# A tile's gates added into the table by indirect DMAs, and a longer lead

## The chip, the cores and the metric

The kernel runs on one core of a Trainium2 chip. The metric is the device time in microseconds; the other cores of the chip are not used.

## The reference

One transformer block over 512 tokens of width 1024, in float32. First a mixer: modulation by a conditioning vector, sliding-window attention of 8 heads beside an mLSTM of 4 heads, an output projection and a residual. Then the part that takes most of the time, the PEER layer: every token picks 128 of 16384 experts (16 in each of 8 heads).

```python
q = (ht @ w_q).reshape(T, 8, 2, 128)
s1, s2 = einsum(q[:, :, 0], keys1), einsum(q[:, :, 1], keys2)   # (T, 8, 128) each
v1, i1 = top_k(s1, 16); v2, i2 = top_k(s2, 16)
cand = v1[..., :, None] + v2[..., None, :]                      # 256 a head
top, pos = top_k(cand, 16)
eidx = (i1 * 128 + i2) at pos                                   # experts, distinct within a head
gate = softmax(top)
act = gelu(einsum('thkd,td->thk', u[eidx], ht)) * gate
y = einsum('thk,thkd->td', act, v[eidx])
```

`u` and `v` are tables of 16384 rows of 1024 floats, 64 MB each. Two heads of a token may choose the same expert; their gates then add up. A second residual with a modulated norm ends the block.

## The kernel before

The first part (up to line 1350) is the mixer and the query scores. `peer_block`, line 1353, is the rest. It splits the tokens. For 192 of them (tile 0 and half of tile 1) the rows of `u` and `v` that they chose are gathered from HBM by indirect DMAs, a row for each of 128 partitions at a time: 384 gathers of 512 KB (`NROWS`), each followed by one VectorE instruction, a dot product for `u` (L1798), a multiply-add for `v` (L1807). The gathers are issued by GpSimd at L1527 into a ring of six buffers, each when VectorE has finished the row six before.

For the other 320 tokens (`TD`, the hot tokens) TensorE computes with all experts. The tables are cut into 128 blocks of 128 experts. A u block is transposed (L1641, L1703) and multiplied with the tokens in three products of split floats: high half with high and low half of the tokens (L1656), low half with the high one (L1660). ScalarE takes the gelu of the scores (L1551). That is multiplied with the gates of the block, a dense table of 128 experts by 320 tokens that is zero where an expert was not chosen, and goes against the v block (L1716 to L1731).

The work is laid out in turns. In the **lead**, turns 0 to 55 (`LEAD` = 56), there are only u blocks; their gelu goes to a table in HBM (`gelu_table`). In the **middle**, turns 56 to 127, each turn does a u block and a v block. In the **tail**, turns 128 to 185, the v blocks that belong to the lead are done, with gelu rows read back (`s_in`). So every block taken into the lead adds one turn to the lead and one to the tail and takes one from the middle.

The lead is long since the gates must be ready before the first v block. VectorE searches the four tiles of 128 tokens one after the other (`for t in range(NT)`), each with the order of its instructions written out, and between them puts the work of the turns by a planner's clock (`beside`, `lead_block`). `SEL_AT` says at which turn a tile's gates are settled. The gates of the hot tokens are then made by TensorE: `turn_choice` transposes keys and gates of a tile, `hot_rows` (VectorE, L1834 and L1838) builds one-hot rows for four tokens, `gates` (TensorE, L1668) multiplies them into a 128 by 128 table for each of the four tokens, `stage_gates` (ScalarE, L1558) copies it, and SP stores it to `gate_table` in HBM (L1468). There are 80 such steps (`GSTEPS`), spread over turns 27 to 50. From there SP loads the gates of eight blocks at a time (L1457) into two buffers.

The low half of a u block in the lead is made in one of two ways: TensorE subtracts the high half in PSUM (L1649) and ScalarE copies, or VectorE subtracts (L1845), for the turns in `LOW_BY_DVE`. `ROWS_LEAD` and `ROWS_TAIL` say how many of the gathered rows are taken in lead and tail: 34 and 68; the middle has the other 282. On SP's queue (L1460 to L1507) stand, in order, u loads, table stores, v loads, gate and gelu loads, each behind its wait, in rings of four.

Of the kernel before, what the change touches and what calls it, by code (L numbers as in the profile page):

```python
# [59 lines left out]
GSTEPS = TD // GT  # L60
TB = 20
NTB = TD // TB
BG = 8
NBG = NBLK // BG
# [24 lines left out]


def tile_of(m):
    return 1 if m < STEPS_OF[1] else 2 if m < STEPS_OF[1] + STEPS_OF[2] else 3

# [7 lines left out]
def gate_steps():  # L101

    steps, m = [[] for _ in range(LEAD)], 0
    ends = {1: SEL_AT[2], 2: SEL_AT[3], 3: G_END}
    for t in (1, 2, 3):
        for it, n in spread(STEPS_OF[t], range(SEL_AT[t] + 1, ends[t] + 1)).items():
            steps[it] = list(range(m, m + n))
            m += n
    return steps


def rows_by_turn():

    n = dict.fromkeys(range(END), 0)
    n |= spread(ROWS_LEAD[0], range(SEL_AT[0] + 2, SEL_AT[3] + 1))
    n |= spread(ROWS_LEAD[1], range(SEL_AT[3] + 1, G_END + 2))
# [5 lines left out]
STEPS, ROWS_AT = gate_steps(), rows_by_turn()  # L122
TURN_OF = [turn for turn in range(END) for _ in range(ROWS_AT[turn])]
# [69 lines left out]
def mix_block(nc, A, keep, R_dram):  # L193

    x_sb, hT, ident, cols, gg2 = keep["x"], keep["hT"], keep["ident"], keep["cols"], keep["gg2"]
    with ExitStack() as ctx:
# [48 lines left out]
        mod_sum = sb("mod_sum", [P, 4, 512])  # L245
        bias_if = sb("bias_if", [MH, 2])
# [60 lines left out]
        block = ctx.enter_context(nc.Block())  # L307

# [93 lines left out]
        def _(pool):  # L402
# [9 lines left out]
            nc.gpsimd.memset(zeros, 0.0).then_inc(S["consts"], 1)  # L412
            nc.gpsimd.memset(v_ext[:, :, :, MV:MV + 1], 1.0).then_inc(S["consts"], 1)
# [18 lines left out]
        CONSTS = 5  # L432
# [920 lines left out]
def peer_block(nc, A, keep, s_all, S_dram, G_dram, out):  # L1353
# [4 lines left out]
    with ExitStack() as ctx:  # L1358
# [6 lines left out]
        def sems(name, n):  # L1365
# [16 lines left out]
        gbuf = stage.rearrange("p g i t -> p g (i t)").rearrange("p g (q b t) -> p g q b t", q=NTB, b=BG)  # L1382
# [15 lines left out]
        chosen_u = sb("chosen_u", [P, 2, K], U32)  # L1398
        tsum = sb("tsum", [P, 2, NT, PH])
        sel = sb("sel", [P, NT - 1, 2, K])  # L1400
        selT = keep["lot"][:, 2 * NBLK * TB:2 * NBLK * TB + 3 * TD].rearrange("p (i t) -> p i t", i=3)
# [47 lines left out]
        def _(sp):  # L1449
# [11 lines left out]
            for it in range(LEAD):  # L1461
# [48 lines left out]
        def _(pool):  # L1510
            nc.gpsimd.iota(iota_i[:], pattern=[[1, P]], base=0, channel_multiplier=0).then_inc(iota_ready, 1)
            pool.wait_ge(eidx_ready, 1)
            for j in range(NROWS):
                if j == EIDX_B_AT:

                    pool.wait_ge(eidx_ready, 2)
                    pool.dma_start(eidx[NB:P, K:K + KB], chosen_u[0:NB, 0, KB:K]).then_inc(eidx_b_in, 16)
                if j == K:
                    pool.wait_ge(eidx_b_in, 16)
                if j == K + 1:  # L1520

                    pool.wait_ge(sel_ready, 2)
# [8 lines left out]
        def _(act):  # L1531
# [33 lines left out]
            func(minus_one[:], ident[:], ACT.Copy, scale=-1.0).then_inc(consts, 1)  # L1565
            lead_high(0)
            lead_low(0)
            for it in range(LEAD):
# [5 lines left out]
                for t in range(NT):  # L1574
                    if it == SEL_AT[t] - 1:
                        act.wait_ge(top_ready, t + 1)
# [5 lines left out]
            for n in range(LEAD, END):  # L1582
# [3 lines left out]
                if n < NBLK:  # L1586
                    act.wait_ge(half_turned, n - LEAD + 1)
                    act.wait_ge(u_done, n)
                    func(H[:, 0, 0:512], ps[:, 6 + n % 2, :], ACT.Copy).then_inc(ua_high, 1)
# [35 lines left out]
        def _(pe):  # L1625
# [19 lines left out]
            def lead_less(n):  # L1645

                pe.wait_ge(u_high, n + 1)
# [24 lines left out]
            def turn_choice(t):  # L1672

                pe.wait_ge(sel_ready, t + 1)
# [6 lines left out]
            pe.wait_ge(consts, 1)  # L1681
            lead_turn(0)
            lead_less(0)
            for it in range(LEAD):
                if it + 1 < LEAD:
                    lead_turn(it + 1)
                pe.wait_ge(u_high, it + 1)
# [9 lines left out]
                for t in range(1, NT):  # L1697
# [37 lines left out]
            for n in range(LEAD, END):  # L1735
# [14 lines left out]
                if n < NBLK:  # L1750
                    pe.wait_ge(ua_high, n - LEAD + 1)
                    pe.wait_ge(ub_high, n - LEAD + 1)
                    pe.wait_ge(ua_low, n - LEAD + 1)
                    scores_high(6 + n % 2, 0)
                    pe.wait_ge(ub_low, n - LEAD + 1)
# [8 lines left out]
        def _(dve):  # L1764
            v = nc.vector
            step = Chain(dve, chain)
            dve.wait_ge(iota_ready, 1)
            step(v.tensor_copy(iota[:], iota_i[:]))
# [41 lines left out]
            def settle(t):  # L1810

                tops, s = top[:, t, :, :], lambda i: tsum[:, i, t, :]
                dve.wait_ge(gate_exp, t + 1)
# [27 lines left out]
            def lead_low(n):  # L1841

                b = n % 2
                dve.wait_ge(u_high, n + 1)
# [215 lines left out]
```

## Time and profile before

| | us |
|---|---|
| median of three runs | 1567.31 (1566.09 to 1570.01) |
| span of the profiled execution | 1563.7 |
| TensorE busy | 1512.8 (97%) |
| VectorE busy | 1401.7 (90%) |
| ScalarE busy | 596.5 (38%) |
| GpSimd busy | 493.3 (32%) |
| moved by DMA | 455.71 MB, mean 291 GB/s |

The span runs from the first to the last instruction of one execution; the profile gives that execution no time of its own beside it. The shares are means over stages with different limits, so they are read again stage by stage. The kernel's three stages of blocks begin at about 392, 742 and 1330 us.

### The profile page before, as it was taken

The numbers are of one execution on the slowest core, as the hardware profiler recorded it, in microseconds if no ns is written. First come the engines' busy times: TensorE is split into PE (matmuls) and PEld (weight loads), VectorE is DVE, ScalarE is ACT, GpSimd is POOL, SyncE is SP. The second block draws the span as 40 slices with busy tenths as digits, with TensorE's granted clock in tenths as the row PEclk, the third lists the DMA queues.
The fourth block names the chain that finished last, engine by engine and source line by source line (L and its number), as shares of the span: only waits on it lengthen the run. The fifth ranks groups of instructions, "written<-read, shape, count | busy, mean of one in ns | idle before, by whom it ended". The sixth has DMA issues, their size and how long they took to land.

```text
span 1563.7 us, 23267 instructions
## 1 busy us (share of the span) xinstructions
PE 1512.8 (97%) x8404; PEld 1281.7 (82%) x8404; DVE 1401.7 (90%) x2988; ACT 596.5 (38%) x968; POOL 493.3 (32%) x422
## 2 busy tenths in 40 slices
PE   7999999899999999999999999999999999999996
PEld 5455654788899999999898999999999899787885
DVE  5887987799999999995999999999999999989997
ACT  3104431521555445543333333333333333334343
POOL 1000000232010411010555565555555555343330
PEclk9999999999999999999999999999999999999998
DMA  9864232230465788789999999999999999999993
GB/s 325 287 217 148 101 138 59 81 98 38 136 212 154 261 262 256 251 278 313 408 396 396 402 401 410 407 397 398 399 407 404 385 402 375 362 406 377 398 391 121
DMA packets 180570, 455.71 MB, mean 291 GB/s; under 512 B 15020, under 2 KB 81700, under 8 KB 178280
## 3 DMA queue, kind: packets, MB, share of 16 engines
q1 hardware_dynamic: 113600, 231.84, 41.2%
q0 software_dynamic: 57632, 209.78, 34.9%
q10 hardware_dynamic: 9224, 12.62, 2.4%
q8 instruction: 67, 1.10, 0.3%
q14 instruction: 47, 0.39, 0.1%
HBM read 421.63 MB, written 32.25 MB: 290 GB/s over the span
## 4 chain that ended last, share of the span: by engine, by line
PE 55%; DVE 13%; DMA 4%; issue 2%; ACT 1%; DVEq 0%; SPq 0%; POOL 0%; ACTq 0%; POOLq 0%
PE peer_psum L1656 13%; PE peer_psum L1660 7%; PE peer_psum L1716 6%; PE peer_psum L1723 6%; PE peer_psum L1731 6%; PE peer_psum L1668 4%; PE peer_psum L1703 3%; PE peer_psum L1720 3%; PE peer_psum L1726 3%; DVE s_all L1807 2%; DMA s_all<-in_peer_v 2%; PE peer_psum L1641 1%; DVE s_all L1902 1%; DVE s_in L1906 1%; DVE s_all L1904 1%
## 5 line engine op out<-in xcount | busy, mean ns | idle before, releaser
L1656 PE MATMUL peer_psum<-hH,hi_slots 128*128 128x320 f32 x1024 | 307.3, 314 | 5.1 <-ACT hi_slots L1599 2.1
L1656 PE MATMUL peer_psum<-hL,hi_slots 128*128 128x320 f32 x1024 | 302.0, 309 | 0.0
L1527 POOL DMA_INDIRECT hT<-in_peer_u,eidx x128 | 146.6, 1145 | 292.0 <-DVE dots L1798 251.5
L1563 ACT ACTIVATE hi_slots<-s_all 128x1024 fp32r<-128x1024 f32 x128 | 135.9, 1062 | 189.2 <-PE peer_psum L1731 172.0
L1527 POOL DMA_INDIRECT hT<-in_peer_v,eidx x128 | 149.6, 1169 | 177.6 <-DVE s_all L1807 164.7
L1656 PEld LDWEIGHTS peer_psum<-hH,hi_slots 128*128 128x128 f32 x1024 | 192.6, 188 | 9.7 <-issue 5.2
L1656 PEld LDWEIGHTS peer_psum<-hL,hi_slots 128*128 128x128 f32 x1024 | 192.6, 188 | 3.1 <-issue 0.2
L1660 PE MATMUL peer_psum<-hH,lo_slots 128*128 128x320 f32 x1024 | 171.2, 309 | 2.1 <-DVE lo_slots L1845 2.1
L1935 DVE TENSOR_TENSOR lo_slots<-s_all,hi_slots 128x1024 fp32r<-128x1024 f32 x128 | 156.3, 1221 | 17.5 <-ACT hi_slots L1563 15.9
L1807 DVE SCALAR_TENSOR_TENSOR s_all<-hT,coef,s_all 128x1024 f32<-128x1024 f32 x126 | 161.3, 1280 | 3.3 <-DMA hT<-in_peer_v,eidx 2.9
L1660 PEld LDWEIGHTS peer_psum<-hH,lo_slots 128*128 128x128 f32 x1024 | 156.6, 188 | 5.1 <-DVE lo_slots L1845 2.6
L1798 DVE CUSTOM_DVE_ANT_0 hT<-hT,lot 128x1024 f32<-128x1024 f32 x128 | 155.8, 1219 | 2.2 <-DMA hT<-in_peer_u,eidx 2.1
L1716 PE MATMUL peer_psum<-hi_slots,a_hi_lo 128*128 128x512 f32 x512 | 147.0, 408 | 4.7 <-ACT a_hi_lo L1596 4.7
L1551 ACT ACTIVATE s_all<-peer_psum 128x320 f32<-128x320 f32 x128 | 56.1, 438 | 244.5 <-PE peer_psum L1660 237.6
L1731 PE MATMUL peer_psum<-lo_slots,a_hi_lo 128*128 128x512 f32 x512 | 140.1, 394 | 0.0
L1723 PE MATMUL peer_psum<-hi_slots,a_hi_lo 128*128 128x512 f32 x512 | 140.1, 394 | 0.0
L1723 PEld LDWEIGHTS peer_psum<-hi_slots,a_hi_lo 128*128 128x128 f32 x512 | 99.0, 193 | 20.9
L1731 PEld LDWEIGHTS peer_psum<-lo_slots,a_hi_lo 128*128 128x128 f32 x512 | 99.0, 193 | 20.4
L1527 POOL DMA_INDIRECT more_rows<-in_peer_u,eidx x64 | 73.7, 1151 | 132.0 <-DVE dots L1798 128.9
L1596 ACT ACTIVATE a_hi_lo<-s_all 128x320 fp32r<-128x320 f32 x128 | 63.7, 497 | 128.9 <-DVE s_all L1961 98.5
L1716 PEld LDWEIGHTS peer_psum<-hi_slots,a_hi_lo 128*128 128x128 f32 x512 | 93.5, 194 | 21.4 <-issue 4.5
L1527 POOL DMA_INDIRECT more_rows<-in_peer_v,eidx x64 | 76.7, 1199 | 67.3 <-DVE s_all L1807 61.2
(318 smaller groups left out, 2856.6 us busy)
## 6 DMA issues: line engine op xcount, KB each, us to landing
ring<-in_peer_u SPq DMA_DIRECT2D x128, 512.0 KB
s_all<-in_peer_v SPq DMA_DIRECT2D x128, 512.0 KB
gate_table<-lot SPq DMA_DIRECT2D x16, 1280.0 KB, 7.1
lot<-gate_table SPq DMA_DIRECT2D x16, 1280.0 KB
gelu_table<-s_all ACTq DMA_DIRECT2D x56, 160.0 KB
s_in<-gelu_table SPq DMA_DIRECT2D x56, 160.0 KB
x_sb<-in_w_mod POOLq DMA_DIRECT2D x8, 1024.0 KB, 8.2
lot<-in_peer_wq SPq DMA_DIRECT2D x8, 1024.0 KB, 5.6
```

Of the source, the lines that this page charges most:

```text
L1527: pool.indirect_dma_start(rows_of(j), None, A[table][0], bass.IndirectOffsetOnAxis(eidx[:, k:k + 1], 0)).then_inc(rows_in[j % RG], 16)
L1563: func(H[:, slot_of(w), :], vb[:, w % RING, :], ACT.Copy).then_inc(v_hi, 1)
L1596: func(aHL[:, w % 2, :, 0], a[:, w % 2, :], ACT.Copy).then_inc(a_hi, 1)
L1656: mm(ps[:, bank, 0:TD], H[:, b, c * P:(c + 1) * P], h[:, c, T0:T], start=(c == 0 and h is hH), stop=False)
L1660: last = mm(ps[:, bank, 0:TD], L[:, b, c * P:(c + 1) * P], hH[:, c, T0:T], start=False, stop=(c == DC - 1))
L1668: last = mm(ps[:, 6 + m % 2, :].rearrange("p (i t) -> p t i", t=GT)[:, k, :], onehot[:, m % NHOT, k, 0, :], onehot[:, m % NHOT, k, 1, :], ...
L1716: mm(y_bank(g, h), aH[:, NB + g * P:NB + (g + 1) * P], H[:, s, h * 512:(h + 1) * 512], start=first, stop=False)
L1723: mm(y_bank(g, h), aL[:, NB + g * P:NB + (g + 1) * P], H[:, s, h * 512:(h + 1) * 512], start=False, stop=False)
L1731: last = mm(y_bank(g, h), aH[:, NB + g * P:NB + (g + 1) * P], L[:, s, h * 512:(h + 1) * 512], start=False, stop=final)
L1798: v.tensor_tensor_reduce(out=rows_of(j), in0=rows_of(j), in1=(h_rows if j < K else keep["h_rows_b"]), scale=1.0, scalar=0.0, op0=ALU.mult, ...
L1807: v.scalar_tensor_tensor(out=y0[:, i, :], in0=rows_of(j), scalar=c, in1=y0[:, i, :], op0=ALU.mult, op1=ALU.add).then_inc(row_done, 1)
L1935: v.tensor_tensor(L[:, s, :], vb[:, w % RING, :], H[:, s, :].bitcast(F32), ALU.subtract).then_inc(v_lo, 1)
```

## The change

Tile 3 is searched first (order 3, 0, 1, 2), and its gates no longer go through the one-hot products. Its part of `gate_table` is filled with zeros during the mixer, VectorE computes for each of its 128 x 128 choices the place in the table, and GpSimd adds the gates there with 128 indirect DMAs of 128 single floats, between its gathers. Within a head the places are distinct; between heads GpSimd waits until all earlier adds have landed. The steps fall from 80 to 48, the lead grows from 56 to 72 blocks, 62 rows are taken in the lead, 97 in the tail and 225 in the middle. The table is stored in pieces of 16 tokens instead of 20.

```diff
-TB = 20
+TB = 16
+SCATTERED = (3,)
+HOT_TOKENS = NB + (SCATTERED[0] - 2) * P
+GSTEPS = HOT_TOKENS // GT
+NTB_HOT = HOT_TOKENS // TB
-LEAD = 56
-SEL_AT = {0: 12, 1: 26, 2: 32, 3: 39}
+LEAD = 72
+SEL_ORDER = (3, 0, 1, 2)
+SEL_AT = {3: 11, 0: 19, 1: 27, 2: 40}
-LOW_BY_DVE = [n for n in range(LEAD) if 25 <= n < 35 or n >= 40]
+LOW_BY_DVE = [n for n in range(LEAD) if 28 <= n < 32 or n >= 41]
-ROWS_LEAD, ROWS_TAIL = (24, 10), 68
+ROWS_LEAD, ROWS_TAIL = (28, 34), 97
-FIN = NBLK + 4
+FIN = NBLK + 27
-STEPS_OF = {1: NB // GT, 2: P // GT, 3: P // GT}
-EIDX_B_AT = RG
+STEPS_OF = {t: (NB if t == 1 else P) // GT for t in range(1, SCATTERED[0])}
+EIDX_B_AT = 16
+ADDS_FIRST = 20
+ADDS_AT = {j: ADDS_FIRST if j == 0 else (K - ADDS_FIRST) * j // (ROWS_IN_LEAD - 1) - (K - ADDS_FIRST) * (j - 1) // (ROWS_IN_LEAD - 1)
+           for j in range(ROWS_IN_LEAD)}
...
+            nc.gpsimd.memset(nothing[:], 0.0).then_inc(S["consts"], 1)
...
+            pool.wait_ge(S["consts"], CONSTS)
+            for g in range(NBG):
+                span = (NTB - NTB_HOT) * BG * TB
+                pool.dma_start(G_table[g, :, NTB_HOT:NTB, :].rearrange("p q n -> p (q n)").rearrange("p (k n) -> p k n", n=512),
+                               nothing[:].unsqueeze(1).broadcast_to([P, span // 512, 512])).then_inc(keep["g_zeroed"], 16)
...
-                if it == G_END + 2:
-                    for i in range(2):
-                        sp.wait_ge(g_stored[i], 16 * (NTB // 2))
-                    load_g(0)
                 if it >= LEAD - 2:
                     sp.wait_ge(g_full, GSTEPS)
                     load_v(it - LEAD + 2)
 
             for w in range(2, RING):
                 load_v(w)
+            for i in range(2):
+                sp.wait_ge(g_stored[i], 16 * (NTB_HOT // 2))
+            for t in SCATTERED:
+                sp.wait_ge(g_added[t], 16 * K)
+            load_g(0)
             load_g(1)
...
+            def add_gates(n):
+
+                nonlocal added
+                for _ in range(n):
+                    h, k = added // PTOP, added % PTOP
+                    if k == 0 and h:
+                        pool.wait_ge(g_added[t], 16 * PTOP * h)
+                    pool.indirect_dma_start(G_flat, bass.IndirectOffsetOnAxis(g_index[:, 0, added:added + 1], 0),
+                                            top[:, t, h, k:k + 1], None, compute_op=ALU.add).then_inc(g_added[t], 16)
+                    added += 1
+
+            pool.wait_ge(keep["g_zeroed"], 16 * NBG)
+            pool.wait_ge(sel_ready, SEL_ORDER.index(t) + 1)
+            add_gates(ADDS_AT[0])
             pool.wait_ge(eidx_ready, 1)
             for j in range(NROWS):
+                if j:
+                    add_gates(ADDS_AT.get(j, 0))
...
+                    if t in SCATTERED:
+                        span = GROUP_SPAN - BG * TB
+                        part = lambda op, by: step(v.tensor_scalar(chosen_u[:, 1, :], ids, by, None, op))
+                        part(ALU.bitwise_and, PK - 1)
+                        step(v.tensor_scalar(g_place[:], chosen_u[:, 1, :], float(NTB * BG * TB), lane_at[:, 0:1], ALU.mult, ALU.add))
...
+                        part(ALU.logical_shift_right, 7)
+                        step(v.scalar_tensor_tensor(out=g_place[:], in0=chosen_u[:, 1, :], scalar=float(TB), in1=g_place[:],
+                                                    op0=ALU.mult, op1=ALU.add))
+                        part(ALU.logical_shift_right, 10)
+                        step(v.scalar_tensor_tensor(out=g_place[:], in0=chosen_u[:, 1, :], scalar=float(span), in1=g_place[:],
+                                                    op0=ALU.mult, op1=ALU.add))
+                        step(v.tensor_copy(g_index[:, SCATTERED.index(t), :], g_place[:]))
```

Left out here: the same search order on the other engines, semaphores that were merged (`ua_high` and `ub_high` into `half_high`, the low ones likewise, with the same waits), a separate tile for the experts of tile 1, and five small instructions at VectorE's start that compute each partition's place.

## Rows read from the trace of the kernel before

**Rows 1.** The page, part 2: busy tenths of TensorE and GB/s, 40 slices.

```profile
PE   7999999899999999999999999999999999999996
...
GB/s 325 287 217 148 101 138 59 81 98 38 136 212 154 261 262 256 251 278 313 408 396 396 402 401 410 407 397 398 399 407 404 385 402 375 362 406 377 398 391 121
```

**Rows 2.** Windows by stage: us; busy us of each engine (instructions); granted clock, DMA share, GB/s.

```profile
392.00:742.00 350.00, 340.73 (x2508) 333.83 (x2509) 317.88 (x951) 172.94 (x236) 46.51 (x42) 1.00 0.73 236
742.00:1330.00 588.00, 582.86 (x3438) 530.17 (x3437) 561.87 (x802) 221.14 (x364) 323.93 (x283) 1.00 1.01 399
1330.00:1560.00 230.00, 216.88 (x920) 175.05 (x918) 207.28 (x274) 90.05 (x130) 77.52 (x62) 0.99 0.90 345
```

**Rows 3.** Timeline of TensorE in the lead, lines of L1660: start us, us.

```profile
400.80 1.34 PE L1660 MATMUL peer_psum<-hH,lo_slots 128*128 128x320 f32 x8
...
480.76 1.34 PE L1660 MATMUL peer_psum<-hH,lo_slots 128*128 128x320 f32 x8
...
485.62 1.34 PE L1660 MATMUL peer_psum<-hH,lo_slots 128*128 128x320 f32 x8
...
716.26 1.34 PE L1660 MATMUL peer_psum<-hH,lo_slots 128*128 128x320 f32 x8
...
723.46 1.34 PE L1660 MATMUL peer_psum<-hH,lo_slots 128*128 128x320 f32 x8
...
727.85 1.34 PE L1660 MATMUL peer_psum<-hH,lo_slots 128*128 128x320 f32 x8
...
740.16 1.34 PE L1660 MATMUL peer_psum<-hH,lo_slots 128*128 128x320 f32 x8
```

**Rows 4.** Chain of waits in middle and tail: start us, us, what.

```profile
1241.32 2.34 PE peer_psum L1656 x16
...
1249.45 2.34 PE peer_psum L1656 x16
...
1465.31 0.93 PE peer_psum L1731 x4
...
1469.03 0.93 PE peer_psum L1731 x4
```

**Rows 5.** Groups by line: busy us, mean ns; VectorE's part of the gates.

```profile
L1838 DVE TENSOR_SCALAR s_all<-iota,lot 128x128 f32<-128x128 f32 x320 | 88.8, 341 | 0.0
...
L1834 DVE TENSOR_TENSOR s_all<-iota,lot 128x512 f32<-128x512 f32 x80 | 54.6, 683 | 1.4 <-PE peer_psum L1668 1.3
```

**Rows 6.** Timeline of VectorE in the middle: start us, us, instruction.

```profile
1266.61 1.28 DVE L1807 SCALAR_TENSOR_TENSOR s_all<-more_rows,coef,s_all 128x1024 f32<-128x1024 f32 x1
1267.80 1.22 DVE L1935 TENSOR_TENSOR lo_slots<-s_all,hi_slots 128x1024 fp32r<-128x1024 f32 x1
1268.94 1.28 DVE L1807 SCALAR_TENSOR_TENSOR s_all<-more_rows,coef,s_all 128x1024 f32<-128x1024 f32 x1
```

**Rows 7.** Windows of 20 us, columns as in Rows 2.

```profile
810.00:830.00 20.00, 19.50 (x118) 17.52 (x117) 18.05 (x30) 7.07 (x12) 10.75 (x10) 1.00 1.02 413
1350.00:1370.00 20.00, 17.85 (x76) 13.86 (x75) 19.58 (x34) 6.70 (x10) 9.79 (x6) 1.00 0.93 334
1370.00:1390.00 20.00, 20.00 (x86) 16.16 (x85) 19.14 (x23) 8.49 (x11) 8.45 (x8) 1.00 1.03 408
```

**Rows 8.** Chain of waits in the tail: a v block on its way.

```profile
1391.80 15.71 DMA s_all<-in_peer_v
```

**Rows 9.** Groups by line: the gathers that GpSimd issues.

```profile
L1527 POOL DMA_INDIRECT hT<-in_peer_u,eidx x128 | 146.6, 1145 | 292.0 <-DVE dots L1798 251.5 <-DVE eidx L1910 36.6 <-issue 4.0
```

**Rows 10.** DMA queues in the first 30 us: packets, MB, share.

```profile
q0 software_dynamic: 96, 0.00, 2.0%
```

**Rows 11.** Timelines of SP and VectorE at the start of the middle.

```profile
731.02 0.33 SPq L1457 DMA_DIRECT2D lot<-gate_table  x1
...
736.40 0.45 SPq L1457 DMA_DIRECT2D lot<-gate_table  x1
...
749.45 0.48 DVE L1961 TENSOR_TENSOR s_all<-s_all,lot 128x320 f32<-128x320 f32 x1
```

More of the change, by code:

```diff
@@ L103, in gate_steps @@
     steps, m = [[] for _ in range(LEAD)], 0
-    ends = {1: SEL_AT[2], 2: SEL_AT[3], 3: G_END}
-    for t in (1, 2, 3):
+    ends = {t: SEL_AT.get(t + 1) if t + 1 in STEPS_OF else G_END for t in STEPS_OF}
+    for t in STEPS_OF:
         for it, n in spread(STEPS_OF[t], range(SEL_AT[t] + 1, ends[t] + 1)).items():
@@ L114, in rows_by_turn @@
     n = dict.fromkeys(range(END), 0)
-    n |= spread(ROWS_LEAD[0], range(SEL_AT[0] + 2, SEL_AT[3] + 1))
-    n |= spread(ROWS_LEAD[1], range(SEL_AT[3] + 1, G_END + 2))
+    n |= spread(ROWS_LEAD[0], range(SEL_AT[0] + 2, SEL_LAST + 1))
+    n |= spread(ROWS_LEAD[1], range(SEL_LAST + 1, G_END + 2))
     n |= spread(NROWS - sum(ROWS_LEAD) - ROWS_TAIL, range(LEAD, NBLK))
@@ L122 @@
 STEPS, ROWS_AT = gate_steps(), rows_by_turn()
+ROWS_IN_LEAD = sum(ROWS_LEAD)
+ADDS_FIRST = 20
+ADDS_AT = {j: ADDS_FIRST if j == 0 else (K - ADDS_FIRST) * j // (ROWS_IN_LEAD - 1) - (K - ADDS_FIRST) * (j - 1) // (ROWS_IN_LEAD - 1)
+           for j in range(ROWS_IN_LEAD)}
 TURN_OF = [turn for turn in range(END) for _ in range(ROWS_AT[turn])]
@@ L245, in mix_block @@
         mod_sum = sb("mod_sum", [P, 4, 512])
+        nothing = sb("nothing", [P, 512])
         bias_if = sb("bias_if", [MH, 2])
@@ L1381, in peer_block @@
         stage = keep["lot"][:, 0:2 * NBLK * TB].rearrange("p (b n t) -> p b n t", b=2, n=NBLK)
-        gbuf = stage.rearrange("p g i t -> p g (i t)").rearrange("p g (q b t) -> p g q b t", q=NTB, b=BG)
+        gbuf = keep["lot"][:, 0:2 * BG * TD].rearrange("p (g q b t) -> p g q b t", g=2, q=NTB, b=BG)
         more_rows = sb("more_rows", [P, RG - 4, D])
@@ L1520, in _ @@
                 if j == K + 1:
-                    pool.wait_ge(sel_ready, 2)
+                    pool.wait_ge(sel_ready, SEL_ORDER.index(1) + 1)
                     pool.dma_start(gate_b[NB:P, :], top[0:NB, 1, :, :].rearrange("p h k -> p (h k)")[:, KB:K]).then_inc(eidx_b_in, 16)
@@ L1573, in _ @@
                 gelu(it, 4 + it % 2)
-                for t in range(NT):
+                for i, t in enumerate(SEL_ORDER):
                     if it == SEL_AT[t] - 1:
-                        act.wait_ge(top_ready, t + 1)
+                        act.wait_ge(top_ready, i + 1)
                         func(top[:, t, :, :], top[:, t, :, :], ACT.Exp).then_inc(gate_exp, 1)
@@ L1672, in turn_choice @@
             def turn_choice(t):
-                pe.wait_ge(sel_ready, t + 1)
+                pe.wait_ge(sel_ready, SEL_ORDER.index(t) + 1)
                 pe.wait_ge(g_staged, sum(STEPS_OF[k] for k in range(1, t)))
@@ L1696, in _ @@
                     gates(m)
-                for t in range(1, NT):
+                for t in STEPS_OF:
                     if it == SEL_AT[t]:
@@ L1766, in _ @@
             step = Chain(dve, chain)
-            dve.wait_ge(iota_ready, 1)
-            step(v.tensor_copy(iota[:], iota_i[:]))
+            dve.wait_ge(iota_ready, 2)
+            step.put(v.tensor_copy(iota[:], iota_i[:]))
+            step(v.tensor_scalar(lane[:, 1:2], lane[:, 0:1], TB - 1, None, ALU.bitwise_and))
+            step(v.tensor_copy(lane_at[:], lane[:]))
+            first = (NTB_HOT * BG) * TB
+            step(v.tensor_scalar(lane_at[:, 0:1], lane_at[:, 0:1], float(BG), float(first), ALU.mult, ALU.add))
+            step(v.scalar_tensor_tensor(out=lane_at[:, 0:1], in0=lane_at[:, 1:2], scalar=1.0 - BG, in1=lane_at[:, 0:1],
+                                        op0=ALU.mult, op1=ALU.add))
             rest = pool_a[:, 4 * D:4 * D + NT * P].rearrange("p (t n) -> p t n", t=NT)
@@ L1812, in settle @@
                 tops, s = top[:, t, :, :], lambda i: tsum[:, i, t, :]
-                dve.wait_ge(gate_exp, t + 1)
+                dve.wait_ge(gate_exp, SEL_ORDER.index(t) + 1)
                 step(v.tensor_reduce(s(0), tops, AX, ALU.add))
@@ L1862, in lead_block @@
                         clock += 0.8
-                    if t and it == SEL_AT[t] + 1:
+                    if t in STEPS_OF and it == SEL_AT[t] + 1:
                         choice_turned(t)
@@ L1878, in beside @@
                     lead_block()
-            for t in range(NT):
+            for t in SEL_ORDER:
                 cap = SEL_AT[t]
@@ L1911, in _ @@
                 else:
-                    if t == 2:
-                        dve.wait_ge(eidx_b_in, 16)
-                    ins = v.tensor_copy(chosen_u[:, 0, :], slots)
+                    ids = chosen_b[:] if t == 1 else chosen_u[:, 0, :]
+                    ins = v.tensor_copy(ids, slots)
                     if t == 1:
```

73 lines of the change are left out of this document (42 added, 31 removed).

## The prediction

> **What bounds the kernel now.** I read the page first: TensorE is busy in 97% of the span and the last 22 of the 40 slices move close to 400 GB/s [rows 1]. One share over a kernel of several stages says little, so I cut the span by stage [rows 2]: up to 392 us attention, mLSTM and the query scores, which the change leaves alone but for some fills; 392 to 742 the lead (u blocks only, the search, the gates); 742 to 1330 the middle (u and v blocks, most gathered rows); 1330 to 1560 the tail (v blocks). In the middle TensorE has 583 of 588 us and the DMA engines are at 1.01, 399 GB/s: two bounds at the same height.
>
> The price of a block is the distance between two like instructions. In the lead [rows 3] a block whose low half VectorE makes takes 723.46 to 727.85, 4.39 us; one that uses TensorE's subtraction 4.86 us, so 0.47 more; a turn with three steps of the gates 7.20 us, so 0.94 a step. In the chain of waits [rows 4] a turn of the middle takes 8.13 us and one of the tail 3.72 us. These are TensorE's own sums, so what TensorE is spared is worth its full time wherever nothing else is late.
>
> **The change, part by part.**
> *Gates of tile 3.* 80 steps become 48: 32 x 0.94 = -30.0 us on TensorE. VectorE loses 32 steps of one 0.683 and four 0.341 us instructions [rows 5], 66 us as durations; as neighbours overlap at their ends (a row of 1.28 us is followed after 1.19, [rows 6]), I take 52 us; ScalarE loses 32 copies. Both lie beside TensorE.
> *Sixteen blocks moved* out of the middle into lead and tail: 16 x (4.39 + 3.72 - 8.13) = -0.3 us. Of the lead's blocks 37 of 72 instead of 30 of 56 use TensorE's subtraction: 7 x 0.47 = +3.3 us.
> *Stalls in the lead.* From block 0's last product to block 55's [rows 3] are 339.4 us. The work is 54 x 4.39 + 3.5 + 29 x 0.47 + 80 x 0.94 = 329.4, so about 10 us are waits, most of them where four searches and the early low halves press VectorE (turn 25) and where four or five steps a turn stand (32 to 40). After the change a turn has one or two steps, VectorE loses 52 us in the lead and gets back 28 rows, nine low halves and some index arithmetic, about 45 us, in a stage 38 us longer (16 x 4.39 - 30 + 3.3 - 5). I leave 5 of the 10 us (bounds: all of it goes, or 5 come on top): -5 us.
> TensorE together: -30.0 - 0.3 + 3.3 - 5 = -32 us.
>
> *DMA, tail.* A turn loads v (0.524 MB), an eighth of a gate table and a gelu row block (0.164 each) and now 97 rows over 73 turns instead of 68 over 57, at 0.524 MB a row: 1.48 MB become 1.55 MB. At 3.72 us that is 397 GB/s before and 416 after. In 20 us pieces [rows 7] the engines give 413 and 408 where their share is over 1; six pieces of that kind in the tail lie at 396 to 408, mean 403. 1.55 MB at 403 to 404 take 3.83 us, 0.11 too much, in some 69 turns: +8 us. The tail already stops on a v block of 15.7 us [rows 8], just the four turns that its ring covers. Bounds: 0 (the spare of the last turns absorbs it) and 69 x 0.27 = +19 us at the 388 GB/s that the tail averages with its dips.
> *DMA, middle.* 225 rows over 56 turns are 4.02 a turn against 3.92: 3.32 MB in 8.13 us, 408 GB/s against 402 now. Full pieces give about 407; the stage's mean of 399 [rows 2] would make it 56 x 0.19 = +11 us. I take +3.
> The Trainium skill ("DMA: Bandwidth & Descriptors", Where 436 GB/s comes from) puts the ceiling of the fabric at 435 GB/s; by it 416 GB/s would fit, both DMA terms would be 0 and the sum 11 us lower. No 20 us piece of this trace is above 413, so the trace decides for the terms as they stand; the case without them is the first rival.
>
> *VectorE in middle and tail.* Rows start 1.2 us apart, a low half takes 1.14, the two small products 0.4 each [rows 6]. A tail turn has 1.33 rows: 1.6 + 1.14 + 0.8 = 3.55 us against 3.72: covered, with 0.17 to spare (0.35 before). If that cover went, each 0.1 us a turn would cost 7 us.
>
> *The 128 indirect adds.* GpSimd issues a gather in 1.15 us [rows 9]; I take the same for an add. 20 go first, then 108 among 61 gathers, 1.77 a gather: 3.2 us a row, against 3.7 us a row that VectorE wants in turns 21 to 40 (28 rows) and 4.2 after. Seven waits between the heads, some 3 us each, fit in the ring's six rows. What stands behind a waiting add on GpSimd is the next gather, and behind that VectorE's row, low halves and steps. Cost 0 if so. On the DMA engines an add is 128 pieces of 4 bytes that are read, added to and written. Nearest rows: in the first 30 us three small GpSimd DMAs make 96 packets in 2.0% of 16 x 30 us [rows 10], 0.10 us a packet, and their 500-odd elements were plainly merged. Merged adds are about two packets per engine and add: 128 x 2 x 0.1 = 26 us per engine. Unmerged they are eight, and a read-modify-write may take two or three times as long: 100 to 300 us. The lead's share is 0.73 [rows 2]; with 72 u blocks, 68 rows, 12 table stores and 72 gelu rows, 98 MB in 378 us (259 GB/s against 236), it is near 0.8, so 75 to 90 us are free. I take the merged case, 0.
> *Other parts.* The table's 8.4 MB of zeros leave from about 145 us, when TensorE is bound by itself and the engines are a third busy: 0, at most +3. Two gate loads start the middle; the first moves from 731.0 behind four v loads and the wait for the adds, to where the second is now, 736.4, with its first reader at 749.5 [rows 11]. Ahead of it stand some 3.4 MB, 9 to 10 us: 0, at most +5. The last add belongs to row 61, due about eight turns before, so SP should not wait for it (behind it stand the u loads of the middle). A few 0.2 us instructions more at VectorE's start: +0.5 us.
>
> *Sum.* -32 + 8 + 3 + 0.5 = -20.5 us against the profiled span of 1563.7, so 1543.2. The page gives no time of its own for that execution; the median of the three runs, 1567.3, is 3.6 us above the span, and I carry this: **1546.8 us**.
>
> **The rivals.**
> A. *Nothing given back to DMA.* The rings absorb the extra rows. For: hardly any wait on a DMA in the middle. Against: 416 GB/s is above every piece. 1567 - 32 = 1535; with all lead stalls gone 1530.
> B. *DMA takes most of it:* middle at 399 and tail at 388 GB/s, +30 instead of +11: 1565, between faster and the same. For: the tail already stops twice. Against: full pieces give over 400.
> C. *The adds fill the DMA engines of the lead: slower.* Each add puts eight separate read-modify-write packets on every engine, gathers and u loads queue behind them, VectorE waits for rows and TensorE for low halves. 1024 packets per engine against 80 to 90 us free: it decides from about 0.1 us a packet, where the 20 us of gain are gone. At 0.15 us they take 154 us, 69 more than is free: about 1615 us. For: small GpSimd packets cost 0.1 us above. Against: they were merged, and the waits between heads spread them. The Trainium skill (same page, Specifications) says that below 512 bytes the engines do a read-modify-write; no row here shows its price, so it bears on this rival alone.
> D. *The change doesn't remove the stage's time:* TensorE is spared, but rows in the lead come late because GpSimd is at 3.2 of 3.7 us; the stalls double instead of halving (+15 on the forecast): 1562, within the noise.
>
> **How the numbers follow.** A measurement of this kernel can tell 0.3%, 4.7 us: faster is below 1562.6, slower above 1572.0. Forecast (1538 to 1556) 0.49; A 0.17; B and D together 0.19, of which 0.12 faster, 0.06 the same and 0.01 slower; C 0.15, of which 0.01 the same. That gives faster 0.78, same 0.07, slower 0.15. The range 1526 to 1572 holds all but C and the far ends of A.
>
> **What would show it.** Right: lead blocks of 4.39 and 4.86 us and single steps near 0.9; the lead some 38 us longer, the middle about 130 us shorter (16 turns of 8.13), the tail 60 to 68 us longer; tail turns of 3.8 us with a share over 1.0. Wrong: turns of 3.72 us throughout the tail (A); GpSimd's gathers in the lead waiting on adds, windows of the lead at a share of 1.0 with few GB/s, block distances over 6 us there (C); the middle's turn above 8.25 us (B).

## The result, and the profile after

The changed kernel takes 1630.62 us (median of 4 runs, 1626.96 to 1639.74) against 1566.88 us beside it: ratio 1.0415, 95% interval [1.0383, 1.0446]. It is 64 us slower; I had forecast 20 us faster, and the time lies outside the range. The profiled execution has a span of 1625.2 us.

The page of the changed kernel, parts 1, 2, 4 and 5; part 2 answers to [rows 1].

```profile
PE 1509.1 (93%) x8159; PEld 1271.0 (78%) x8159; DVE 1344.9 (83%) x2811; ACT 585.3 (36%) x927; POOL 744.7 (46%) x568
...
PE   7999999999999387879889999999999999999997
...
PEclk9999999999999798999999999999999999999998
...
PE 30%; POOL 18%; DVE 11%; DMA 9%; issue 6%; ACT 1%; DVEq 0%; SPq 0%; ACTq 0%; POOLq 0%
...
L1545 POOL DMA_INDIRECT gate_table<-top,g_index x128 | 219.6, 1716 | 140.2 <-DVE top L1862 82.3
L1844 DVE CUSTOM_DVE_ANT_0 hT<-hT,lot 128x1024 f32<-128x1024 f32 x128 | 156.0, 1219 | 101.5 <-DMA hT<-in_peer_u,eidx 101.4
...
L1702 PE MATMUL peer_psum<-hH,lo_slots 128*128 128x320 f32 x1024 | 178.2, 318 | 33.6 <-DVE lo_slots L1891 33.6
...
L1844 DVE CUSTOM_DVE_ANT_0 more_rows<-more_rows,lot 128x1024 f32<-128x1024 f32 x64 | 78.0, 1219 | 47.6 <-DMA more_rows<-in_peer_u,eidx 47.6
```

TensorE, nearly full in every slice of [rows 1] after the first, has gaps from slice 14 on (it was busy for 97%, now 93). L1545 is the new add: 1.716 us of GpSimd each. The products of VectorE with gathered rows (L1844) wait 149 us in all for their rows (7 us in the kernel before), and the low products (L1702) wait 33.6 us for low halves that VectorE makes.

The stages of the changed kernel, in the columns of [rows 2]; behind the three stages stands the 20 us window in which TensorE stood almost still.

```profile
400.00:866.00 466.00, 396.24 (x2729) 384.98 (x2729) 306.89 (x824) 180.74 (x238) 296.54 (x197) 0.93 0.75 211
866.00:1323.00 457.00, 450.03 (x2661) 409.22 (x2660) 436.89 (x631) 170.28 (x280) 265.31 (x223) 1.00 1.02 401
1323.00:1609.00 286.00, 280.21 (x1189) 227.02 (x1188) 269.10 (x333) 113.69 (x152) 124.10 (x94) 0.99 0.98 384
540.00:560.00 20.00, 2.47 (x12) 2.47 (x13) 5.82 (x12) 0.00 (x0) 16.65 (x12) 0.50 0.52 111
```

And the timeline of its TensorE at L1702, as [rows 3]: blocks 0, 27, 28, 71 and the last of the middle, then the last value product (L1772).

```profile
400.87 1.33 PE L1702 MATMUL peer_psum<-hH,lo_slots 128*128 128x320 f32 x8
...
532.38 1.34 PE L1702 MATMUL peer_psum<-hH,lo_slots 128*128 128x320 f32 x8
...
563.28 1.43 PE L1702 MATMUL peer_psum<-hH,lo_slots 128*128 128x320 f32 x8
...
866.23 1.33 PE L1702 MATMUL peer_psum<-hH,lo_slots 128*128 128x320 f32 x8
...
1322.81 1.33 PE L1702 MATMUL peer_psum<-hH,lo_slots 128*128 128x320 f32 x8
...
1608.77 1.10 PE L1772 MATMUL peer_psum<-lo_slots,a_hi_lo 128*128 128x512 f32 x4
```

| stage | before | after | change | forecast |
|---|---|---|---|---|
| lead, block 0 to the last | 339.4 | 465.4 | +126.0 | +38 |
| middle | 584.6 | 456.6 | -128.0 | -127 |
| tail | 222.2 | 286.0 | +63.8 | +60 to 68 |

Middle and tail came as forecast; all 88 us that are missing lie in the lead. Block 28 follows block 27 after 30.9 us, and after it distances of 8 to 15 us stand among the regular 5.28 (4.39 + 0.88 for one step). The reason can be read where GpSimd reaches its first row. GpSimd's timeline of the changed kernel, first two adds and first rows:

```profile
475.63 2.48 POOL L1545 DMA_INDIRECT gate_table<-top,g_index  x1 [82.27 <-DVE top L1862]
478.40 1.57 POOL L1545 DMA_INDIRECT gate_table<-top,g_index  x1 [0.30 <-issue]
...
517.41 1.01 POOL L1569 DMA_INDIRECT hT<-in_peer_u,eidx  x1 [0.31 <-issue]
518.73 1.59 POOL L1545 DMA_INDIRECT gate_table<-top,g_index  x1 [0.30 <-issue]
520.62 1.00 POOL L1569 DMA_INDIRECT hT<-in_peer_u,eidx  x1 [0.30 <-issue]
521.92 1.58 POOL L1545 DMA_INDIRECT gate_table<-top,g_index  x1 [0.30 <-issue]
523.81 1.59 POOL L1545 DMA_INDIRECT gate_table<-top,g_index  x1 [0.30 <-issue]
525.70 0.99 POOL L1569 DMA_INDIRECT hT<-in_peer_u,eidx  x1 [0.30 <-issue]
```

But for the waits between heads GpSimd never rests: between any two instructions there are only the 0.30 us called "issue", time in which the engine waited for nothing that the profile shows. An add costs 1.716 + 0.30 = 2.02 us, a row 1.13 + 0.30 = 1.43. The waits between heads are 21 us in all, 19 without the 0.30 of each: 128 x 2.02 + 62 x 1.43 + 19 = 366 us (61 rows and one small move), which is the time from the first add (475.6) to the end of the last (841.7). Of the chain of waits between 475 and 842 us L1545 holds 53.6%, issue 14.6% and the two groups of gathers 16.1%. VectorE's timeline of the changed kernel shows the other side, each of its first rows waited for:

```profile
522.75 1.23 DVE L1844 CUSTOM_DVE_ANT_0 hT<-hT,lot 128x1024 f32<-128x1024 f32 x1 [8.52 <-DMA hT<-in_peer_u,eidx]
527.32 1.23 DVE L1844 CUSTOM_DVE_ANT_0 hT<-hT,lot 128x1024 f32<-128x1024 f32 x1 [3.34 <-DMA hT<-in_peer_u,eidx]
...
535.67 1.23 DVE L1844 CUSTOM_DVE_ANT_0 hT<-hT,lot 128x1024 f32<-128x1024 f32 x1 [3.24 <-DMA hT<-in_peer_u,eidx]
```

The releaser is named "DMA", since VectorE waits for a gathered row to land. The first wait, 8.5 us, says when VectorE was ready: at 514.2. The DMA engines were not full (share 0.75 in the lead): the gather had been issued late. To know which of the two it is, GpSimd's time or the traffic of the adds, experiments are needed. Theory G: GpSimd's own time is the loss. Theory D (the mechanism of rival C): the small read-modify-write packets are.

### The profile page after: what moved, and what is told of

Same layout as the page of the kernel before. It is cut to its first block, busy times and chain, and to the rows that moved or that the text cites. A ratio compares the mean times of both kernels' runs of the same rounds, so it can differ in the third digit from the quotient of the medians.

```text
span 1625.2 us, 22693 instructions
## 1 busy us (share of the span) xinstructions
PE 1509.1 (93%) x8159; PEld 1271.0 (78%) x8159; DVE 1344.9 (83%) x2811; ACT 585.3 (36%) x927; POOL 744.7 (46%) x568
## 2 busy tenths in 40 slices
DMA packets 197655, 460.99 MB, mean 284 GB/s; under 512 B 34156, under 2 KB 96740, under 8 KB 195368
## 4 chain that ended last, share of the span: by engine, by line
PE 30%; POOL 18%; DVE 11%; DMA 9%; issue 6%; ACT 1%; DVEq 0%; SPq 0%; ACTq 0%; POOLq 0%
POOL gate_table L1545 12%; PE peer_psum L1698 7%; PE peer_psum L1757 4%; PE peer_psum L1764 4%; PE peer_psum L1772 4%; POOL hT L1569 4%; PE peer_psum L1702 3%; DMA s_all<-in_peer_v 3%; DVE s_all L1853 2%; DMA gate_table<-top,g_index 2%; PE peer_psum L1761 2%; PE peer_psum L1744 2%; PE peer_psum L1767 2%; POOL more_rows L1569 2%; DMA hT<-in_peer_v,eidx 2%
## 5 line engine op out<-in xcount | busy, mean ns | idle before, releaser
L1545 POOL DMA_INDIRECT gate_table<-top,g_index x128 | 219.6, 1716 | 140.2 <-DVE top L1862 82.3
L1844 DVE CUSTOM_DVE_ANT_0 hT<-hT,lot 128x1024 f32<-128x1024 f32 x128 | 156.0, 1219 | 101.5 <-DMA hT<-in_peer_u,eidx 101.4
L1569 POOL DMA_INDIRECT hT<-in_peer_v,eidx x128 | 160.6, 1255 | 158.9 <-DVE s_all L1853 140.9
L1702 PE MATMUL peer_psum<-hH,lo_slots 128*128 128x320 f32 x1024 | 178.2, 318 | 33.6 <-DVE lo_slots L1891 33.6
L1702 PEld LDWEIGHTS peer_psum<-hH,lo_slots 128*128 128x128 f32 x1024 | 161.5, 194 | 40.0 <-DVE lo_slots L1891 36.7
L1772 PE MATMUL peer_psum<-lo_slots,a_hi_lo 128*128 128x512 f32 x512 | 140.1, 394 | 0.0
L1844 DVE CUSTOM_DVE_ANT_0 more_rows<-more_rows,lot 128x1024 f32<-128x1024 f32 x64 | 78.0, 1219 | 47.6 <-DMA more_rows<-in_peer_u,eidx 47.6
L1299 POOL TENSOR_TENSOR wqL<-lot,wqH 128x2048 fp32r<-128x2048 f32 x7 | 32.2, 4604 | 184.5 <-DVE wqL L1316 140.5
L1764 PEld LDWEIGHTS peer_psum<-hi_slots,a_hi_lo 128*128 128x128 f32 x512 | 99.6, 195 | 20.9
L1569 POOL DMA_INDIRECT more_rows<-in_peer_v,eidx x64 | 83.2, 1299 | 70.5 <-DVE s_all L1853 63.5
L1772 PEld LDWEIGHTS peer_psum<-lo_slots,a_hi_lo 128*128 128x128 f32 x512 | 99.1, 194 | 20.5
```

The lines of the kernel that those rows point to most:

```text
L1545: pool.indirect_dma_start(G_flat, bass.IndirectOffsetOnAxis(g_index[:, 0, added:added + 1], 0), top[:, t, h, k:k + 1], None, compute_op=AL ...
L1569: pool.indirect_dma_start(rows_of(j), None, A[table][0], bass.IndirectOffsetOnAxis(eidx[:, k:k + 1], 0)).then_inc(rows_in[j % RG], 16)
L1702: last = mm(ps[:, bank, 0:TD], L[:, b, c * P:(c + 1) * P], hH[:, c, T0:T], start=False, stop=(c == DC - 1))
L1764: mm(y_bank(g, h), aL[:, NB + g * P:NB + (g + 1) * P], H[:, s, h * 512:(h + 1) * 512], start=False, stop=False)
L1772: last = mm(y_bank(g, h), aH[:, NB + g * P:NB + (g + 1) * P], L[:, s, h * 512:(h + 1) * 512], start=False, stop=final)
L1844: v.tensor_tensor_reduce(out=rows_of(j), in0=rows_of(j), in1=(h_rows if j < K else keep["h_rows_b"]), scale=1.0, scalar=0.0, op0=ALU.mult, ...
```

## The experiments

The kernel before ran on the same chips at 1564.17 us (first four), 1562.95 (next four) and 1566.64 (last four). "Lead" is block 0 to the last block of the lead.

**1. No adds.** The call at L1545 and the waits for it go, so tile 3's gates stay zero.

```
-                    pool.indirect_dma_start(G_flat, ..., compute_op=ALU.add).then_inc(g_added[t], 16)
-                sp.wait_ge(g_added[t], 16 * K)
```

> Leaves out: the 128 indirect adds of tile 3's gates and the waits for them (its gates stay zero). All else is the changed kernel. Theory G (GpSimd's own time: an add holds it 1.72 us and 0.30 us pass to the next instruction, so the stream of 128 adds and 62 gathers paces the lead from 475 to 842 us): the lead falls from 465 us to 375 to 385, the total to 1535 to 1550. Theory D (the adds' small packets fill the DMA engines): the same here. Theory S (the longer lead with its other split of rows costs by itself): stays above 1600.

1539.83 us, ratio 0.9846 [0.9826, 0.9866]; lead 373.0 us (402.88 to 775.89). The adds cost 1630.6 - 1539.8 = 91 us, all of it in the lead (92.4 us there): without them the kernel is 24.3 us faster than the one before, near the 20.5 of the forecast.

**2. GpSimd busy without a DMA, first size.** Four memsets in place of an add; tile 3's gates are left out.

```
-                    pool.indirect_dma_start(G_flat, ..., compute_op=ALU.add).then_inc(g_added[t], 16)
+                    for _ in range(4):
+                        idle_step(nc.gpsimd.memset(idle[:], 0.0))
```

> Leaves out the adds as before, but where one stood GpSimd clears a small scratch tile four times, each waiting for the last, about 2.0 us with no DMA at all. Theory G: the lead is slow again, 440 to 480 us, total 1600 to 1640. Theory D: as without adds, 1535 to 1550.

1546.41 us, ratio 0.9883 [0.9863, 0.9903]. This missed what I expected under G, but the dummy was mis-sized: four memsets took 1.22 us, not 2, and with 1.3 to 1.7 us in each add's place GpSimd nearly keeps up (lead 379.5 us). Run 5 repeats it with the right size.

**3. Plain scatter.** The same DMAs without `compute_op`: gates overwrite instead of adding, so of two heads with the same expert one gate is lost.

> The 128 indirect DMAs write the gates plainly instead of adding them (experts chosen by two heads keep one gate). Theory G with the price in making the descriptors: 1.5 us or more an instruction as before, total 1610 to 1630. Theory G with the price in the add: an instruction costs 1.15 us like a gather, total 1555 to 1575. Theory D: the read-modify-write is gone, the DMA share in the lead falls and at least 40 us come back even if GpSimd's instructions stay as long.

1571.97 us, ratio 1.0037 [1.0011, 1.0062]; the eight runs spread from 1560.6 to 1581.5, more than in any other experiment, and the profiled one, with a lead of 405.7, is the longest. The group of the scatter in this kernel, and in experiment 4:

```profile
L1545 POOL DMA_INDIRECT gate_table<-top,g_index x128 | 160.9, 1257 | 134.7 <-DVE top L1862 82.3 <-issue 36.9 <-DMA gate_table<-top,g_index 15.6
```

Without the addition GpSimd needs 1.257 us an instruction, and the loss falls from 91 to 32 us. The packets fall at the same time, from 144 an add to 32 (below), and 59 us came back where I had written "at least 40" under D, so this run does not tell G from D.

**4. Half of each add.** Partitions 0 to 63 alone, 64 gates an instruction; the other half of tile 3's gates stays zero.

```
-   IndirectOffsetOnAxis(g_index[:, 0, added:added + 1], 0), top[:, t, h, k:k + 1]
+   IndirectOffsetOnAxis(g_index[0:64, 0, added:added + 1], 0), top[0:64, t, h, k:k + 1]
```

> Each of the 128 adds takes 64 partitions instead of 128 (the gates of half of tile 3's tokens stay zero): half the pieces, as many instructions. Theory G, price by instruction: 1.6 us each, total 1610 to 1630. Theory G, price by piece: about 0.9 us each, 110 us of GpSimd less, total 1550 to 1570. Theory D: half the packets, half the loss, about 1585 whatever GpSimd's instructions take.

1619.88 us, ratio 1.0353 [1.0324, 1.0381]; lead 447.1.

```profile
L1545 POOL DMA_INDIRECT gate_table<-top,g_index x128 | 205.8, 1608 | 136.0 <-DVE top L1862 82.3 <-issue 36.9 <-DMA gate_table<-top,g_index 16.9
```

Half of the pieces save 6% of the instruction and 11 of the 91 us: the price hangs on the number of instructions.

**5. GpSimd busy without a DMA, right size.** Six memsets, 1.9 us; tile 3's gates are left out.

> Like the changed kernel, but each of the 128 adds is replaced by six chained memsets of 128x192 on GpSimd (0.33 us each by the run with four of them, so about 2.0 us where an add and its gap take 2.02); no gate of these 128 tokens is added and nobody waits for one, so tile 3's gates are left out. Theory G (GpSimd's own time is the loss): the stretch from 475 us to the last of them is as long as with adds, near 370 us, VectorE waits for gathered rows again, lead block 0 to 71 takes 440 to 470 us, and the time is 1600 to 1630. Theory D (the adds' packets or their traffic are the loss): no packets, so 1540 to 1550.

1616.85 us, ratio 1.0337 [1.0295, 1.0379]; lead 448.2. Its window 480 to 560, and then the same window of the version without adds:

```profile
480.00:560.00 80.00, 60.03 (x407) 58.39 (x406) 47.16 (x132) 34.41 (x41) 64.95 (x215) 0.88 0.50 163
```

```profile
480.00:560.00 80.00, 79.84 (x571) 78.31 (x570) 69.73 (x185) 43.65 (x54) 27.66 (x22) 1.00 0.77 270
```

With no packet of an add on the DMA engines (share 0.50) TensorE loses 20 us here, where the change loses 24, and 75 of the 92 us in the lead are lost again. The stretch from the first to the last memset is 347 us, 19 less than the 366 with adds: the waits between heads, 21 us, are the part that this kernel leaves out.

**6. The packets without GpSimd.** No adds; SyncE's queue writes 128 times one gate of 128 tokens, to other places than the reference wants.

```
+                    sp.dma_start(G_dram[i % NBG, :, NTB_HOT, i // NBG:i // NBG + 1],
+                                 top[:, 3, i // PTOP, i % PTOP:i % PTOP + 1], ...).then_inc(g_added[3], 16)
```

> Like the changed kernel without its adds, but SyncE's queue issues 128 plain DMAs in turns 22 to 69, each writing one gate of 128 tokens as 128 separate pieces of 4 bytes into the table; the gates land in other places than the reference wants, and none is added. So the small packets are there and GpSimd is free. Theory G: 1540 to 1555 (the version without adds took 1539.8). Theory D (small packets cost): 1575 or more; if each of them takes 45 ns as the adds' do, that is 46 us of each DMA engine, of which the lead has some 60 free.

1538.64 us, ratio 0.9837 [0.9796, 0.9877], as without them: 128 plain DMAs of 4-byte pieces cost nothing measurable from SyncE's queue. The pages count 197655 packets here and in the change, 179222 without adds: 144 for each of the 128 DMAs in both. These are writes, not additions, so they do not speak for the dearer packets of an add; run 7 does.

**7. Every second add.** 64 of the 128, in the same places between the rows; half of tile 3's gates are left out.

```
+                    if added % 2:
                         pool.indirect_dma_start(...)
```

> Like the changed kernel, but only every second add is issued (64 of 128, same places between the rows), so half of tile 3's gates are left out. Theory G: GpSimd needs 64 x 2.02 + 62 x 1.5 + 21 = 243 us from 475, so it is done near 718, and a row costs it 3.6 us where 4.1 are there; the loss is gone almost wholly, 1540 to 1560. A loss in proportion to the adds (each costs a fixed share, wherever it lies) would give 1539.8 + 45 = 1585.

1539.09 us, ratio 0.984 [0.9798, 0.9881]. Its window of TensorE's worst stretch, and the one of the changed kernel:

```profile
480.00:560.00 80.00, 80.00 (x572) 78.52 (x571) 68.56 (x183) 43.64 (x55) 63.74 (x43) 1.00 0.83 242
```

```profile
480.00:560.00 80.00, 56.19 (x388) 54.64 (x387) 43.79 (x128) 32.66 (x40) 64.35 (x43) 0.86 0.66 157
```

GpSimd is equally busy in both (64 of 80 us), and yet TensorE loses nothing, since more of that time goes to rows, 19 against 10: a row carries 54/61 = 0.89 adds, at 1.83 + 0.30 us each in this run, so it costs GpSimd 0.89 x 2.13 + 1.5 = 3.4 us, and 3.8 with its share of the waits between heads (what I wrote ahead of the run, 3.6, came by 1.03 adds a row and no waits). The traces have a row every 3.9 us here (495.9 to 732.1), every 5.3 us in the change (517.4 to 841.7), and every 4.2 us without adds (477.7 to 734.4), where GpSimd waits for VectorE. Here 64 adds are free, and 64 more cost 91 us: a threshold, no share for each.

**8. The long lead alone.** The kernel before with `LEAD = 72`, `ROWS_LEAD, ROWS_TAIL = (28, 34), 97`, `FIN = NBLK + 27`.

> The kernel before with the lead of 72 blocks, 62 rows in the lead and 97 in the tail alone; all gates are still built as one-hot products, nothing is scattered. By the terms of the prediction: TensorE subtraction of 16 blocks more on TensorE for VectorE +3.3 or less, DMA in tail and middle +11 at most, lead stalls -5, so 1560 to 1577 against 1565. If it is clearly slower than the version of the change without adds by less than 20 us, the adds replaced less work than the 30 us that I counted for the gate steps; by 25 to 35 us, the term is right.

1574.54 us, ratio 1.0064 [1.0044, 1.0084]; lead 405.6. By itself this part makes the kernel 10 to 12 us slower. The version without adds is 34.7 us below, 32.6 of them in the lead. That is not the price of 32 steps alone, since the two kernels differ in more. By the forecast's terms run 8's lead has 70 x 4.39 + 3.5 + 29 x 0.47 + 80 x 0.94 = 399.6 us of work, so 6 us of stalls, and run 1's has none: -30 for the steps, +3.3 for seven more subtractions on TensorE, -6 for the stalls.

**9 to 11. Half of the scatter.** These compute everything. Only the 64 table tokens of tile 1 are scattered, searched first; slots k and k + 8 of a head share an add (the upper partitions of `g_pack` and `g_index` are filled by three small DMAs), so 64 adds of 128 gates. Tiles 2 and 3 keep their one-hot products, 64 steps.

```
-SCATTERED = (3,)
+SCATTERED = (1,)
-SEL_ORDER = (3, 0, 1, 2)
+SEL_ORDER = (1, 0, 2, 3)
-                    h, k = added // PTOP, added % PTOP
+                    h, k = added // AK, added % AK
...
+                                            g_pack[:, added:added + 1], None, compute_op=ALU.add)
```

With a lead of 56 blocks and the rows of before:

> Computes all of the reference. The scatter is halved and the lead stays at 56 blocks, with the rows as before (34 in the lead, 68 in the tail): only the 64 table tokens of tile 1 are scattered, and two slots of one head and token (k and k+8) share an add, so 64 adds of 128 gates (10 before the first row), after three small moves of indices and gates by DMA; tiles 2 and 3 are built as one-hot products (64 steps instead of 80). Theory G (GpSimd's time, from a threshold): 64 x 2.02 + 34 x 1.5 = 180 us from about 480, done near 680 with the waits, before the lead ends at about 725; so the adds cost nothing and 16 steps fewer bring 15 to 17 us: 1545 to 1555 against 1564. Rival: the adds cost in proportion (46 us for 64, half of the change's 91): 1590 or more.

With 64 blocks, 48 rows in the lead and 82 in the tail:

> Computes all of the reference. As the half scatter with 56 blocks, but a lead of 64 blocks with 48 rows in it and 82 in the tail. The longer lead alone cost 11 us for 16 blocks, so 5 for 8: 1549 to 1560. If a longer lead paid off once the adds are hidden, it would be below the version with 56.

With 72 blocks and the change's rows:

> Computes all of the reference. As the half scatter with 56 blocks, but with the lead of 72, 62 rows in it and 97 in the tail, as in the change. The long lead with all gates as products took 1574.5; 16 steps fewer at 32 for 35 us is 17: 1554 to 1562. GpSimd needs 64 x 2.02 + 62 x 1.5 = 222 us plus waits, as in the run with every second add, where it was hidden; if the loss came back here, 1570 or more.

Measured: 56 blocks 1566.14 us, ratio 0.9991 [0.9973, 1.0009]; 64 blocks 1561.6, 0.9975 [0.9959, 0.9991]; 72 blocks **1558.13 us, 0.9934 [0.9913, 0.9955]**, faster than both kernels. The two sizes of 64 and 56 are worse than I thought, and in the opposite order. The window 480 to 560 of the kernels with 56, 64 and 72 blocks:

```profile
480.00:560.00 80.00, 66.68 (x444) 65.03 (x443) 51.56 (x138) 32.89 (x41) 61.69 (x41) 0.89 0.66 182
```

```profile
480.00:560.00 80.00, 72.36 (x475) 70.54 (x474) 59.27 (x155) 35.33 (x44) 57.99 (x41) 0.91 0.72 205
```

```profile
480.00:560.00 80.00, 75.83 (x533) 73.37 (x532) 64.68 (x176) 40.56 (x52) 61.46 (x42) 0.98 0.78 222
```

TensorE stands for 13.3, 7.6 and 4.2 us. With 56 blocks 54 adds go between 34 rows, 1.64 a row, at 1.75 + 0.30 us each, and the waits between heads are 24.2 us in all: from the first row (509.3) to the end of the last add (688.3) a row takes 5.4 us, no better than the 5.3 of the change. With 64 blocks it is 4.6 us, with 72 blocks 4.1, so near VectorE's own pace. What is left there fits a late start: the first row is issued at 503.6, in run 7 at 495.9, and up to 560 both have a row every 3.5 us; but this kernel also has 16 steps more, and I did not separate the two. I had summed GpSimd's time over the whole lead (it is done at 688, before the lead ends at 741) and not in the turns in which VectorE wants rows: the mistake of the prediction once more, in small. The 15 us of 16 steps went there: that lead lasts 340.1 us, as long as before. With 72 blocks it lasts 394.0, 11.6 less than in run 8.

**12. The adds spread evenly.** `ADDS_FIRST = 2` instead of 20.

> The changed kernel with 2 adds instead of 20 ahead of the first gathered row, and the other 126 spread over the 62 rows. If the first 20 adds, which put off the first row by 37 us, are what costs, the time falls by 20 to 37 us, to 1594 to 1610. If GpSimd's whole stretch of 128 adds and 62 rows is what costs (theory G), its length stays near 372 us from 475 and the time stays within 10 us of the change's: 1620 to 1640.

1639.83 us, ratio 1.0465 [1.0438, 1.0493]; lead 474.7. The first row is issued at 480.2 instead of 517.4, TensorE is busy for 72.0 instead of 56.2 us between 480 and 560, but the last add starts at 847.5 instead of 839.8: the wait moves, and the sum stays, as theory G had it. The 20 first adds decide where TensorE stands, not for how long.

## Why the prediction was wrong

*The step that failed* is "GpSimd issues a gather in 1.15 us; I take the same for an add", with what it led to: "3.2 us a row, against 3.7 us a row that VectorE wants" and "Cost 0 if so"; the adds cost 92 us of the lead. An add takes 1.72 us and GpSimd needs 0.30 us between any two instructions, for rows too: 1.77 x 2.02 + 1.43 = 5.0 us a row, with the waits between heads 5.3, as the trace has it. That is above the 3.7 and the 4.2 us that were wanted. And the lead follows GpSimd: in the change and in runs 3, 4, 5 and 12 the last add or its stand-in ends at 841.7, 787.2, 828.9, 824.2 and 849.0 us, and the lead's last block comes 21 to 27 us behind it each time; in run 7, without the loss, it comes 42 us behind. [rows 9] hides the gap: only 4.0 us of issue stand there for 128 gathers, since nearly each of them waited for something else; it comes out where GpSimd is late. Nor did I bound the add from both sides by time on GpSimd; I bounded only its packets.

*The second omission:* the 20 adds ahead of the first row start when tile 3's gates are settled (475.6 us) and hold it up for 42 us (most distances are 1.86, two are longer, and there is one wait between heads), to 517.4. VectorE was ready for it at 514.2 and had it at 522.7, 5.3 us after the issue, so it had to be issued by 509; in run 1, where it is issued at 477.7, six rows lie ready in the ring. I priced the adds between the rows and let these go. Run 12 shows that their place by itself gains nothing.

*The rivals.* D named the right mechanism, late rows through GpSimd, and priced it at +15 us where the adds cost 92 in the lead; run 5, where nearly the same time on GpSimd without any DMA of the adds gives 1616.9 us, and run 7 show it. C came nearest in time (1615), by luck: its mechanism is not what the runs show. The queue of GpSimd (q0) in the changed kernel and in experiment 3, 480 to 505 us:

```profile
q0 software_dynamic: 1879, 0.01, 21.1%
```

```profile
q0 software_dynamic: 512, 0.01, 1.5%
```

In this window, with adds alone on that queue, a packet takes 0.211 x 16 x 25 us / 1879 = 0.045 us, and 13 adds make 1879 packets, 144 each. So they are unmerged, nine to an engine and add, about as C supposed, but at less than half of the 0.1 us from which it would decide: some 50 us per engine over a lead that had 80 to 90 free. A plain scatter makes 32 packets of 0.012 us, so an add keeps the DMA engines busy for 17 times as long. The Trainium skill ("DMA: Bandwidth & Descriptors", Specifications) says that below 512 bytes the engines do a read-modify-write, and this bore on C. The trace shows a price for adding, 0.045 us a packet, but none for small pieces as such: neither 128 plain DMAs of 144 packets (run 6) nor 64 adds (run 7) cost time.

*Right:* gates, subtractions and stalls of the lead together, -30.0 + 3.3 - 5 = -31.7 against -32.6 measured (runs 8 and 1); the middle, -127 against -128; the tail, +60 to 68 against +63.8; blocks of 4.39 and 4.86 us, single steps of 0.88. Of the stalls in the lead all 10 us go once rows are in time, not 5: 70 x 4.39 + 3.5 + 36 x 0.47 + 48 x 0.94 = 372.8 us, and the version without adds measures 373.0. The terms without the adds gave -20.5 us; run 1 has -24.3.

*DMA.* Sixteen more turns of 3.72 us would have made the tail 59.5 us longer (rival A), with my +8 for DMA 67.5; it grew by 63.8, halfway. And it did not grow as I had it: most of its turns take 3.72 us, and the extra time stands in nine longer ones of 3.9 to 7.4 us, while the 20 us pieces with a full share move 395 to 407 GB/s. So the term had about half its size in the tail, the picture of an evenly longer turn was wrong, and whether the 4 us are DMA or order I did not separate.

*What is left open:* the 17 us between run 5 and the change, which the adds' packets or the waits between heads may cost. The waits between heads (21 us) fit them, but I did not run a version without those waits, as two heads may add to the same place of the table.

## What to carry to other kernels

An engine that only issues DMAs is a resource like the others: count its time with the gap between instructions, in the turns in which its results are wanted, and not over the stage. When an edit puts work ahead of or between the transfers that a full engine waits for, price that work by its own kind; an add took 1.5 times the gather that I took for it. And when the cost has a threshold, try half of the edit before giving it up: half of this scatter with the long lead came out 8.5 us below the kernel before, about a third of the 24 us that the version without adds shows; with the short lead it gained nothing.

## What the runs showed of the hardware

- GpSimd's time for an indirect DMA of 128 pieces, mean of one: gather 1.14 to 1.16 us for rows of u (0.99 to 1.01 for the first ones of the lead), plain scatter 1.257, scatter with addition 1.716; scatter with addition on 64 partitions 1.608, so nearly the same; where only 64 adds are issued, 1.75 to 1.83 each. Between instructions 0.30 us.
- The granted clock: in the lead of the changed kernel it is 0.50 in the window 540 to 560, level 1.2 GHz, after TensorE had stood for most of 532 to 559; the first eight products behind it, from 559.8 us on, start 0.27 us apart instead of 0.15, those from 562.1 on 0.15 again, and the clock is 1.00 in the middle. This stall thus cost about 1 us more than its own length.
- On the DMA engines an accumulating scatter of 128 single floats makes 144 packets of 0.045 us, a plain indirect one 32 packets of 0.012 us.
- 128 plain DMAs of 128 pieces of 4 bytes from SyncE's queue, 144 packets each, between u loads, cost no measurable time (1538.6 against 1539.8 us).
